# A retention head whose value unit, sample output and cached values come before its four new states

## The reference

```
att = einsum('bihd,bjhd->bhij', qc, kc) * dmat
o   = einsum('bhij,bjhe->bihe', att, vc) + einsum('bihd,bhde->bihe', qc, S) * q_decay
S   = chunk_decay * S + einsum('bjhd,bjhe->bhde', kc * k_decay, vc)
```

## Time and profile before

| what | value |
|---|---|
| median of 3 executions | 864.79 us (863.93 to 865.35) |
| profiled execution | 867.8 us, of which the span is 866.1 us |
| busy in the span | PE 844.1, DVE 446.1, ACT 248.4, POOL 206.7 us |
| share of PE in the chain that ended last | 91% |
| mean granted TensorE clock | 0.994 of full speed |

### The profile page before, as it was taken

One profiled execution on the slowest core, in us unless ns is written; L12 is line 12 of the kernel. 1 busy time (PEld: TensorE's weight loads), 2 busy tenths in 40 slices (PEclk: granted clock), 3 DMA queues, 4 the chain that ended last, 5 costly groups with the idle time before them and its releaser, 6 DMA issues.

```text
span 866.1 us, 20033 instructions
## 1 busy us (share of the span) xinstructions
PE 844.1 (97%) x7644; PEld 809.2 (93%) x7644; DVE 446.1 (52%) x799; ACT 248.4 (29%) x370; POOL 206.7 (24%) x181
## 2 busy tenths in 40 slices
PE   7999999999999999999999999999899999999996
PEld 6999999999999999998899797898799999999996
DVE  4437844595438634773545454554463333333467
ACT  4124421441224403342232223312242222222200
POOL 0019301650138002824315105134100000000003
PEclk9999999999999999999999999999989999999998
DMA  6998979876995799677889596796939678877712
GB/s 193 227 273 315 314 206 228 287 270 218 213 354 172 269 203 282 219 259 252 278 311 367 172 388 238 250 370 212 396 118 326 224 268 269 264 268 274 256 49 110
DMA packets 162731, 220.02 MB, mean 254 GB/s; under 512 B 8577, under 2 KB 136321, under 8 KB 160961
## 3 DMA queue, kind: packets, MB, share of 16 engines
q1 hardware_dynamic: 157856, 206.05, 76.0%
q0 software_dynamic: 4176, 11.02, 3.9%
q10 hardware_dynamic: 656, 2.36, 0.7%
HBM read 206.68 MB, written 100.01 MB: 354 GB/s over the span
## 4 chain that ended last, share of the span: by engine, by line
PE 91%; DVE 3%; DMA 2%; issue 1%; ACT 1%; POOL 1%; SPq 0%; POOLq 0%; DVEq 0%; ACTq 0%
PE bank L775 23%; PE bank L777 22%; PE bank L776 22%; PE bank L770 6%; PE bank L805 5%; PE bank L1082 3%; PE bank L900 2%; PE bank L875 2%; PE bank L1134 1%; PE bank L1159 1%; PE bank L1035 1%; PE bank L1122 1%; DMA xn<-in_x_prompt_dram 1%; PE bank L1149 1%; DVE wl L1497 1%
## 5 line engine op out<-in xcount | busy, mean ns | idle before, releaser
L775 PE MATMUL bank<-xh,wh 128*128 128x288 f32 x640 | 193.2, 302 | 0.7 <-DVE vn L1564 0.6
L777 PE MATMUL bank<-xh,wl 128*128 128x288 f32 x640 | 189.5, 296 | 0.0
L776 PE MATMUL bank<-xl,wh 128*128 128x288 f32 x640 | 189.4, 296 | 0.0
L775 PE MATMUL bank<-wh,xh 128*128 128x256 f32 x640 | 184.1, 288 | 1.1 <-DVE wl L1497 0.8
L776 PE MATMUL bank<-wl,xh 128*128 128x256 f32 x640 | 179.4, 280 | 0.0
L777 PE MATMUL bank<-wh,xl 128*128 128x256 f32 x640 | 179.3, 280 | 0.0
L1497 DVE TENSOR_TENSOR wl<-raw,wh 128x1024 fp32r<-128x1024 f32 (+1 forms) x104 | 129.8, 1286 | 9.9 <-ACT wh L1297 9.1
L775 PEld LDWEIGHTS bank<-wh,xh 128*128 128x128 f32 x640 | 121.3, 190 | 4.5 <-issue 2.6
L775 PEld LDWEIGHTS bank<-xh,wh 128*128 128x128 f32 x640 | 121.4, 190 | 1.8 <-issue 1.2
L1297 ACT ACTIVATE wh<-raw 128x1024 fp32r<-128x1024 f32 (+1 forms) x104 | 101.8, 1018 | 74.1 <-PE bank L805 43.5
L776 PEld LDWEIGHTS bank<-xl,wh 128*128 128x128 f32 x640 | 121.5, 190 | 0.1
(11 more groups left out here) (206 smaller groups left out, 1457.8 us busy)
## 6 DMA issues: line engine op xcount, KB each, us to landing
raw<-in_w_in_dram SPq DMA_DIRECT2D x128, 256.0 KB
out_dram<-in_cache_kv_w_dram SPq DMA_DIRECT2D x16, 2040.0 KB, 10.2
out_dram<-in_cache_kv_w_dram SPq DMA_DIRECT2D x32, 1020.0 KB, 9.6
cslot<-in_cache_kv_w_dram SPq DMA_DIRECT2D x24, 1024.0 KB, 8.7
far<-in_cache_kv_w_dram SPq DMA_DIRECT2D x32, 512.0 KB, 9.8
out_dram<-in_cache_kv_w_dram SPq DMA_DIRECT2D x20, 504.0 KB, 10.8
raw<-in_w_in_dram SPq DMA_DIRECT2D x16, 512.0 KB
keyslot<-in_cache_kv_w_dram SPq DMA_DIRECT2D x8, 1024.0 KB, 8.0
```

Of the source, the lines that this page charges most:

```text
L775: pe.matmul(out, lhs[0](k), rhs[0](k), start=(k == 0), stop=False)
L776: pe.matmul(out, lhs[0](k), rhs[1](k), start=False, stop=False)
L777: last = pe.matmul(out, lhs[1](k), rhs[0](k), start=False, stop=(k == n - 1))
```

## The change

The calls of one retention head are put in another order, on PE and, to match, on DVE. `value_unit(4)` moves ahead of the sample's output; `cached_output(0)` comes right behind the sample's output; the first pair of new states follows, then the transposes (`cached_turn(0)` and two key tiles), then the second pair, then the key-query products. On DVE the weight split `low(...)` and the value copy `values(4)` move ahead of the copy of the sample's output, and `output(0)` moves between the two pairs of state updates. ACT, POOL and SP are the same row by row.

```diff
                 b = group(3)
                 blocks(lambda t, c: turn(b[:, c], rot[:, t, RK:2 * RK]))
+                value_unit(4)
                 sample_output()
+                cached_output(0)
                 sample_state_pair(0)
-                value_unit(4)
-                sample_state_pair(2)
-                cached_output(0)
-                att_group()
                 cached_turn(0)
                 transpose_tile(r, 1, 0)
                 transpose_tile(r, 1, 1)
+                sample_state_pair(2)
+                att_group()
                 state_group(0)
                 state_group(1)
...
+                low(C0_C if last else r * B_CH + (C0_B + 2), 0)
+                values(4)
                 sample_output()
                 sample_states(0)
                 sample_states(1)
-                low(C0_C if last else r * B_CH + (C0_B + 2), 0)
-                values(4)
+                output(0)
                 sample_states(2)
                 sample_states(3)
                 attention()
-                output(0)
                 chain(0)
                 chain(1)
```

## The result

The changed kernel takes 873.95 us (median of four, 873.07 to 878.55) against 864.37 for the kernel before: a ratio of 1.0123, 95% interval 1.0091 to 1.0155. It is slower, as forecast, but by 9.6 us and not by 5.4, and outside the range. The profiled execution took 878.55 us with a span of 876.9, 10.8 more than the span before. In what follows a difference written as +x us is the ratio less 1, times 864.4; the ratio is formed over all executions, so it can differ by some tenths of a us from the difference of the two medians.

The account below looks back on a forecast made before the run. PE, busy 844.1 of 866.1 us, was taken as the bound. Per head -0.70 + 0.74 + 1.03 + 0.16 = +1.23 us, four heads +4.9, keys +0.5: +5.4, from 864.79 to 870.2 us; range 867.3 to 873.8.

Parts of the forecast that it names:

- the mechanism in the heads: Bank waits on PE in each retention head: one of 0.70 us goes, 0.74, 1.03 and 0.16 come; +1.23 us a head.
- The third wait: At the second group of chunk states, group 11 waits for group 9's bank to be read: 0.16 us.
- Q + 2.10: Q starts the second pair; DVE returns group 7's bank at Q + 2.10, so key-query products wait 1.03 us.
- The queues behind the states: Later state stores make SP 2.9 us late, so next head's keys hold PE 0.47 us; 0.5 taken once.
- the 0.5 us: PE's wait for late keys in passages from head to head, counted once in the sum.
- the tail-clock rival: In the last head's tail, the clock stays up because the wait behind its fall moves in time; chance 0.06.
- the bounds: PE's wait for keys from head to head: nothing, or 1.87 us in each of three passages, 5.6 in all.
- The late-transfers rival: SP late by 4.3 us; keys or second sequence's cached values hold PE in every passage: 875.3 us; chance 0.10.
- the clock: Rival: the clock falls inside the heads, as the new order idles 0.74, 1.03 and 0.16 us; chance 0.08.

Follow-up runs that it names:

- late copies: Against the changed kernel: SP issues the copies of the last head and of the first feature tile only at the program's end; 869.41 us, ratio 1.0045.
- split keys: Changed order with POOL's rstd ahead of its landing waits, second key tile's transposes moved behind the second pair of states; 870.67 us, ratio 1.0063.
- key tiles first: Kernel before, with both key tiles' transposes on PE between sample's output and first pair of states; 863.34 us, ratio 0.9990; repeated 864.00 us, 0.9986.
- both pairs covered: Changed order with POOL's rstd ahead of landing waits, key tiles before the first pair, cached values between the pairs; 866.32 us, ratio 1.0015.
- `rstd` first: Against the changed kernel: in the last head POOL issues the chunk-state store and computes rstd before waiting for either store's landing; 869.02 us, ratio 1.0058.

## Why the prediction was wrong

**Right: the mechanism in the heads.** The wait of 0.61 us went, and new ones came at the second pair and at the key-query products, for the reason given. The size was nearly half too high: 1.23 us a head was forecast; 0.83 and 0.86 came in the first two, and 0.65 in the last up to its second group of key tiles. The third wait came nearly as forecast (0.19 for 0.16). The hand-off to line 1141 came at Q + 1.94, not Q + 2.10; and the value unit, the sample's output and the cached values ran in 2.83 + 5.48 us (478.57, the start of the transposes, plus the 0.59 that they took before, to 481.99, and on to 487.47) and not 2.99 + 5.57: a piece's length from start to start differs a little with its neighbours. These three make 0.4 us, nearly the whole of the difference. The range allowed 0.3 us a head either way; no run shows that figure, and these three heads came 0.37 to 0.58 us below the 1.23.

**Wrong: "The queues behind the states".** The step that failed is the path: it followed the late stores into SP's queue and stopped there, and put their way through POOL's queue at nothing without a reason. SP's load of the next states came late, as said,

```profile
496.65 0.38 SPq L549 DMA_DIRECT2D st<-in_state_ret_dram  x1
```

3.36 us after the 493.29 of the kernel before, of which 0.8 came from the head ahead; so 2.5 us later in the head (2.9 was forecast), and 1.6 and 1.4 in the first and the third. But the keys never held PE, so the 0.5 us was nothing. POOL's own queue was left out. It carries the stores, two waits for landings, and behind them `rstd`, for which DVE, and behind it PE, waits. In the second head of the change this did no harm:

```profile
497.20 0.58 POOL L731 DMA_DIRECT2D out_dram<-schain  x1 [2.82 <-DVE schain L1817]
508.42 0.23 POOL L738 TENSOR_SCALAR rstd<-bmv 128x4 f32<-128x4 f32 x1 [10.64 <-DVE bmv L1779]
```

The stores had landed in time, `rstd` waited for the statistics, and PE had projection units of the next head to do and took `rot` only at 518.91, without a wait. In the last head there is no next head, and there the trace of before gave a slack of only 2.3 us: the chunk-state store, issued at 611.68, landed in 8.0 us, at 619.7, and `rstd` started at 621.98. With the stores 3.7 us later in the head and both landings longer, PE's wait in the tail grew from 2.32 to 8.4 us: about 6 us. In the tail-clock rival I even wrote that "the wait itself is unchanged". The chain of waits behind every late store had to be followed on every queue, to the last head.

**Wrong: the bounds.** I had read the landing of the state stores as 4.4 us or less, from the first head. In the last head they took longer before too (POOL idle 7.27 us for them). In the loop SP holds its loads until the stores have landed (before, three waits for POOL's line 728, 20.4 us in all and 7.6 the longest); in the last head it does not, and its loads of cached values began at 602.86, beside the stores at 602.97. That these loads are the reason was not tried. The late-transfers rival thus had the wrong victim: keys in the passages between heads, instead of `rstd` at the end.

**Partly right: the clock.** Its rival was given 0.08. The fall in the earlier trace rows lasted nearly 7 us at half of the full clock, and half of that, an estimated 3.4 us at most, was taken as what a fall costs. Falls came inside the heads in 3 of the 20 profiled heads with the changed order (one in the change, one in its repeat, one in the kernel with late copies) and in 2 of the 4 with split keys. There was none in 20 heads of the old order (8 of them with the key tiles first), nor in the 4 of the kernel with both pairs covered. These counts are small. In the change the clock was at 0.50 for about 3.4 us, and this cost 1.5 us, under half of that estimate. Four heads at 3 falls in 20, or at 5 in 24 with the split, make an estimated 0.9 to 1.3 us an execution. With 3.4 for the waits that gives 4.3 to 4.7, and the kernel with `rstd` first measured +5.0 (3.2 to 6.8). The difference between that kernel and the change, 5.6 us (1.0058 against 1.0123), is what the tail costs, in line with the 6.1 of the profiled pair.

The tail's fall did not go away. In the change the clock was at 0.50 from 633.4 to 643.4 (before, from 626.4 to 633.0), and PE stood idle in it until 636.98; from the first transposes of `rot` to the end of the span it is 239.9 us in both kernels, so the fall costs the same. But the fall is not as steady as I took it to be: in the kernel with the old order in the last head it lasted from 628.4 to 631.6 us only. And in three profiles (the repeated change, the old order in the last head, and `rstd` first) the clock was also at 0.50 for 3.3 to 6.8 us in the first 18 us of the program, ahead of all that the change touches. So single executions differ by more than the waits, and the split of the loss in the heads between waits and clock is an estimate.

## What to carry to other kernels

When a change makes something later, follow it on every in-order queue that it sits in, to the last instruction of the queue, and in the last iteration of a loop by itself: there the cover of the next iteration is missing (in the changed kernel's second head PE took `rot` without a wait, in its last head it waited 8.4 us), and loads that a wait held back in the loop may run free (SP's began at 602.86 here, beside the stores at 602.97). A store that nobody reads can still stand before a small instruction that everybody waits for, as the chunk-state store with its 10.1 us to landing stood before `rstd`; issue such an instruction first and wait for landings last (PE's wait was 2.3 us then). And a piece that is moved to cover one wait uncovers what it hid in its old place (0.61 us went here, 0.56 and 0.81 came): list that first.

## What the runs showed that was not expected

A store of 128 KB took 2.5 us to land without copies beside it and 10.1 with them. The granted clock fell to 0.50 of full speed behind two short waits of 0.56 and 0.81 us in some heads and not in others of the same execution, once behind a single wait of 1.00 us, and in none of the 16 profiled heads with one bank wait of 0.6 us. Two pairs of bank waits with nearly the same sum (0.56 and 0.81, or 1.00 and 0.22) did not differ in time by what could be told.
